# Two transformer stacks on one core: the RMS norms' sums of squares per token, in a 128x4 corner

## The reference

```python
def rmsnorm(x, g):
    xf = x.astype(jnp.float32)
    y = xf * lax.rsqrt(jnp.mean(xf * xf, axis=-1, keepdims=True) + EPS)
    return (y * g.astype(jnp.float32)).astype(x.dtype)
```

## Time and profile before

| | |
|---|---|
| median of 3 runs | 2605.52 us (2602.32 to 2605.62) |
| the profiled execution | 2600.53 us, of which the span from the first to the last instruction is 2598.8 us |
| PE busy | 2526.3 us (97%), 11928 matmul records |
| POOL busy | 1782.7 us (69%) |
| DVE busy | 1091.8 us (42%) |
| ACT busy | 578.7 us (22%) |

### The profile page before, as it was taken

One profiled execution on the slowest core, in us unless ns is written; L12 is line 12 of the kernel. 1 busy time (PEld: TensorE's weight loads), 2 busy tenths in 40 slices (PEclk: granted clock), 3 DMA queues, 4 the chain that ended last, 5 costly groups with the idle time before them and its releaser, 6 DMA issues.

```text
span 2598.8 us, 34640 instructions
## 1 busy us (share of the span) xinstructions
PE 2526.3 (97%) x11928; PEld 2032.1 (78%) x11928; DVE 1091.8 (42%) x1626; ACT 578.7 (22%) x992; POOL 1782.7 (69%) x816
## 2 busy tenths in 40 slices
PE   7999999999999899999999999989999999899999
PEld 5877778688888587777868888867888788688887
DVE  3565422544454366543254445456047732311100
ACT  2133222211100213331121111033224520211100
POOL 5766777588888376667758888825452467588887
PEclk9999999999999799999999999989999999999999
DMA  3222222222355122222223225511112122232233
GB/s 122 90 82 83 86 89 93 70 97 96 102 206 185 51 90 81 89 81 89 90 72 97 96 96 204 202 54 53 55 60 90 66 81 91 72 97 96 97 111 101
DMA packets 70213, 250.84 MB, mean 97 GB/s; under 512 B 8304, under 2 KB 8432, under 8 KB 70000
## 3 DMA queue, kind: packets, MB, share of 16 engines
q1 hardware_dynamic: 66816, 241.74, 28.1%
q10 hardware_dynamic: 3312, 7.95, 0.9%
HBM read 247.56 MB, written 2.10 MB: 96 GB/s over the span
## 4 chain that ended last, share of the span: by engine, by line
PE 64%; issue 13%; POOL 12%; DMA 9%; DVE 1%; SPq 0%; ACT 0%; POOLq 0%; DVEq 0%; ACTq 0%
PE bank L475 15%; PE bank L471 15%; PE bank L472 15%; DMA w_raw<-weights 9%; POOL w_lo L397 6%; POOL w_hi L394 5%; PE bank L425 3%; PE bank L426 3%; PE bank L427 3%; PE bank L699 1%; PE bank L1047 1%; PE bank L431 1%; PE bank L432 1%; PE bank L433 1%; PE bank L708 1%
## 5 line engine op out<-in xcount | busy, mean ns | idle before, releaser
L394 POOL TENSOR_TENSOR w_hi<-w_raw,one 128x1024 fp32r<-128x1024 f32 x405 | 778.0, 1921 | 775.2 <-PE bank L475 453.3
L397 POOL TENSOR_TENSOR w_lo<-w_raw,w_hi 128x1024 fp32r<-128x1024 f32 x405 | 1006.4, 2485 | 31.8
L471 PE MATMUL bank<-act_hi,w_hi 128*128 128x512 f32 x1840 | 726.5, 395 | 5.5 <-POOL w_hi L394 5.5
L472 PE MATMUL bank<-act_lo,w_hi 128*128 128x512 f32 x1840 | 717.6, 390 | 0.0
L475 PE MATMUL bank<-act_hi,w_lo 128*128 128x512 f32 x1904 | 472.3, 390 | 0.0
L475 PEld LDWEIGHTS bank<-act_hi,w_lo 128*128 128x128 f32 x1904 | 356.9, 188 | 74.8 <-issue 1.0
L471 PEld LDWEIGHTS bank<-act_hi,w_hi 128*128 128x128 f32 x1840 | 346.1, 188 | 85.6 <-issue 12.9
L472 PEld LDWEIGHTS bank<-act_lo,w_hi 128*128 128x128 f32 x1840 | 346.1, 188 | 75.1 <-issue 3.8
L471 PE MATMUL bank<-f_hi,w_hi 128*128 128x512 f32 x528 | 208.0, 394 | 0.0
L472 PE MATMUL bank<-f_lo,w_hi 128*128 128x512 f32 x528 | 208.0, 394 | 0.0
L475 PE MATMUL bank<-f_hi,w_lo 128*128 128x512 f32 x528 | 134.8, 394 | 0.0
(11 more groups left out here) (396 smaller groups left out, 3393.1 us busy)
## 6 DMA issues: line engine op xcount, KB each, us to landing
w_raw<-weights SPq DMA_DIRECT2D x405, 512.0 KB, 3.4
mod_raw<-mods SPq DMA_DIRECT2D x48, 512.0 KB, 4.3
bias<-bias ACTq DMA_DIRECT2D x8, 512.0 KB, 4.1
resid<-x SPq DMA_DIRECT2D x8, 256.0 KB, 5.2
out<-resid ACTq DMA_DIRECT2D x8, 256.0 KB, 4.2
params<-params ACTq DMA_DIRECT2D x2, 534.5 KB, 3.7
ctx_raw<-ctx SPq DMA_DIRECT2D x1, 1024.0 KB, 4.9
second<-second SPq DMA_DIRECT2D x1, 972.5 KB, 6.9
```

The source lines that it names most:

```text
L394: nc.gpsimd.tensor_tensor(w_hi[:, j, :], w_raw[:, j, :], one[:, 0:1].to_broadcast([P, 1024]), ALU.mult)\
L397: nc.gpsimd.tensor_tensor(w_lo[:, j, :], w_raw[:, j, :], w_hi[:, j, :].bitcast(F32), ALU.subtract).then_inc(blocks_split, 1)
L471: mm(out, w_hi[:, slot, tile * P:tile * P + P], rows_hi, start=start, stop=False)
L472: mm(out, w_hi[:, slot, tile * P:tile * P + P], rows_lo, start=False, stop=False)
```

## The change

The x norms get the y norms' form. `x_norm_sum` makes four fp32 matmuls of four columns in place of one of 512, with the squares as weights. Root and reciprocal are 128x4 (`root_x`, `rroot_x`). DVE builds the diagonals in `spread` and PE spreads them over the partitions with one more matmul (`x_norm_spread`). `apply` and `apply_mod` read the result from `bank[6]`; for the FFN's form ACT copies it to SBUF (`x_rstd_row`), where `ffn_scaled` waits for it. An identity is placed in `bank[7]` at each x norm. The context's sums move to `bank[4]`. In `add_rows` the next `scaled` is issued behind the addition and no longer ahead of it.

```diff
             def x_norm_sum(n, k):
 
+                if k == 0:
+                    nc.tensor.transpose(bank[7][:, P:2 * P], ident, ident).then_inc(x_ident, 1)
                 pe.wait_ge(x_sq, 8 * n + k + 1)
-                mm(bank[7][:, :], ones, squares[k % 2], start=(k == 0), stop=(k == KT - 1)).then_inc(x_summed, 1)
+                for tt in range(TT):
+                    last = mm(bank[7][:, 0:4], squares[k % 2][:, tt * P:tt * P + P], pick[:, 3 - tt:7 - tt],
+                              start=(k == 0 and tt == 0), stop=(k == KT - 1 and tt == TT - 1))
+                last.then_inc(x_summed, 1)
+
+            def x_norm_spread(n):
+
+                pe.wait_ge(x_spread, n + 1)
+                mm(bank[6][:, :], ones, squares[0], start=True, stop=True).then_inc(x_bc, 1)
...
                 first_two(b0, [bank[0][:, :], bank[1][:, :]], lo0, odd, norm=norm)
-                pairs(0, (2, 3))
+                pairs(0, (2,))
+                if norm is not None:
+                    x_norm_spread(norm)
+                pairs(0, (3,))
...
             x_norm_sums(0)
+            x_norm_spread(0)
...
                 mod_sums(28, 4).then_inc(mods_done, 1)
+                x_norm_spread(2 * l + 2)
...
             for k in range(KT):
-                last = mm(bank[6][:, 0:CTX], ones, ctx_sq[:, k, :], start=(k == 0), stop=(k == KT - 1))
+                last = mm(bank[4][:, 0:CTX], ones, ctx_sq[:, k, :], start=(k == 0), stop=(k == KT - 1))
...
             x_norm_sums(2 * DEPTH + 1)
+            x_norm_spread(2 * DEPTH + 1)
...
             def x_norm(n):
                 act.wait_ge(x_summed, 8 * n + 8 + 2)
-                run(root_row, bank[7][:, :], ACT.Sqrt, bias=eps, scale=1.0 / D).then_inc(x_root, 1)
+                run(root_x[:, 0:4], bank[7][:, 0:4], ACT.Sqrt, bias=eps, scale=1.0 / D).then_inc(x_root, 1)
+
+            def x_rstd_row(n):
+
+                act.wait_ge(x_bc, n + 1)
+                run(rstd_row, bank[6][:, :], ACT.Copy).then_inc(x_rstd, 1)
...
             def x_norm_later(n):
 
                 dve.wait_ge(x_root, n + 1)
-                step.inc(v.reciprocal(rstd_row, root_row))
-                return step.value()
+                did(v.reciprocal(rroot_x[:, 0:4], root_x[:, 0:4]))
+                dve.wait_ge(x_ident, n + 1)
+                v.tensor_tensor(x_diag, bank[7][:, P:2 * P].unsqueeze(1).to_broadcast([P, 4, P]),
+                                rroot_x[:, 0:4].unsqueeze(2).to_broadcast([P, 4, P]), ALU.mult).then_inc(x_spread, 1)
 
             def x_norm(n):
-                dve.wait_ge(step.sem, x_norm_later(n))
+                x_norm_later(n)
+                dve.wait_ge(x_bc, n + 1)
...
                 there = scaled(0)
                 for k in range(KT):
-                    following = scaled(k + 1) if k < KT - 1 else None
                     dve.wait_ge(step.sem, there)
                     v.tensor_tensor(resid[:, k, :], resid[:, k, :], tmp[:, k % 4, :], ALU.add).then_inc(x_ready, 1)
-                    there = following
-                    if then is not None and k >= 1:
-                        then(k - 1)
-                if then is not None:
-                    then(KT - 1)
+                    if k < KT - 1:
+                        there = scaled(k + 1)
+                    if then is not None:
+                        then(k)
```

More of the change, by code:

```diff
@@ L157, in build @@
         root_k, rroot_k = keep("root_k", [P, 48]), keep("rroot_k", [P, 48])
+        root_x, rroot_x = root_k[:, 0:4], rroot_k[:, 0:4]
         root_q, rroot_q, q_scale = keep("root_q", [P, 32]), keep("rroot_q", [P, 32]), keep("q_scale", [P, 8, TT])
@@ L215, in build @@
         sum_sq = tmp[:, 2, :]
-        rstd_row, root_row = squares
+        rstd_row = squares[0]
+        x_diag = spread[:, 0:4, :]
         KB = 1024
@@ L297, in build @@
         x_sq, x_summed, x_root = sem("x_sq"), sem("x_summed"), sem("x_root")
+        x_ident, x_spread, x_bc, x_rstd = (sem(n) for n in ("x_ident", "x_spread", "x_bc", "x_rstd"))
         t_ready, hi_ready, lo_ready = sem("t_ready"), sem("hi_ready"), sem("lo_ready")
@@ L1306, in _ @@
                 x_norm(2 * l + 1)
+                x_rstd_row(2 * l + 1)
                 ffn_scaled(BL * l + B_FFN, lambda b: use("ffn", b, 0, l), FT * l)
@@ L1320, in _ @@
             act.wait_ge(ctx_ss, 1)
-            run(root_row_c[:, :], bank[6][:, 0:CTX], ACT.Sqrt, bias=eps, scale=1.0 / D).then_inc(ctx_root, 1)
+            run(root_row_c[:, :], bank[4][:, 0:CTX], ACT.Sqrt, bias=eps, scale=1.0 / D).then_inc(ctx_root, 1)
             def apply_hi_mod(n, shift):
@@ L1562, in apply @@
                         dve.wait_ge(lo_ready, 8 * a + k - 3)
-                    v.scalar_tensor_tensor(tmp[:, k % 4, :], resid[:, k, :], g_pre[:, k:k + 1], rstd_row,
+                    v.scalar_tensor_tensor(tmp[:, k % 4, :], resid[:, k, :], g_pre[:, k:k + 1], bank[6][:, :],
                                            ALU.mult, ALU.mult).then_inc(t_ready, 1)
@@ L1594, in ffn_scaled @@
                         dve.wait_ge(f_lo_ready, f0 + 2 * i + j + 1)
-                        dve.wait_ge(step.sem, rstd_there)
+                        dve.wait_ge(x_rstd, rstd_there)
                         v.tensor_tensor(tmp[:, j, :], bank[2 * j][:, :], rstd_row, ALU.mult)\
@@ L1897, in _ @@
                 add_rows(G_POST_MIX, 16 * l + 8, rows_low)
-                rstd_there = x_norm_later(2 * l + 1)
-                ffn_scaled(rstd_there, BL * l + B_FFN, lambda b: use("ffn", b, 0, l), FT * l)
+                x_norm_later(2 * l + 1)
+                ffn_scaled(l + 1, BL * l + B_FFN, lambda b: use("ffn", b, 0, l), FT * l)
                 dve.wait_ge(f_lo_ready, FT * l + FT + 2)
@@ L1932, in apply_mod @@
                         dve.wait_ge(lo_ready, 8 * a + k - 3)
-                    v.scalar_tensor_tensor(tmp[:, k % 4, :], resid[:, k, :], gain[:, k:k + 1], rstd_row,
+                    v.scalar_tensor_tensor(tmp[:, k % 4, :], resid[:, k, :], gain[:, k:k + 1], bank[6][:, :],
                                            ALU.mult, ALU.mult).then_inc(t_ready, 1)
```

## The result

The changed kernel takes 2622.75 us (median of 4, 2620.34 to 2627.36) against 2603.92 us (median of 4, 2601.86 to 2605.62): a ratio of 1.0075, 95% interval 1.0056 to 1.0093, so it is slower by some 19 us. The prediction was 2625.6 us. The profiled execution took 2627.36 us with a span of 2625.6, 26.8 more than the span of before. It is the slowest of its four, and the profiled execution of before, at 2600.53 us, is faster than the four that its median is taken from, so the two traces lie further apart than the medians do.

The account below looks back on a forecast made before the run. The prediction took PE's stream, with POOL's splitting as partner, to bound the kernel. Terms 3.3 + 3.8 + 2.6 + 5.0 + 5.4 gave +20.1 us, 2625.6 us against the median; 8 in 10 between 2608 and 2642.

Parts of the forecast that it names:

- x norm 2: End of the first layer: sums stay at 1.2 GHz to the end, plus 3.5; chain minus 0.2; +3.3 us in all.
- x norm 0: Start: all eight sums at 1.2 GHz, plus 4.5; chain after them minus 0.7; +3.8 us in all.
- x norm 5: Second block's FFN: half the sums at 0.95, half at 1.71, plus 3.0; chain minus 0.4; +2.6 us in all.
- x norm 4: End of the second layer: slower sums plus 5.9, earlier addition minus 0.5, later context sums plus 1.1, clock minus 1.5; +5.0 us.
- x norms 1 and 3: First block's FFNs: earlier start -0.9, spreading +0.95, identity +0.15, weight loads +0.4, later clock rise +2.1; +2.7 us each.
- The cover that I named: In the first block's FFNs, blocks 2 and 3 cover the banks' later freeing; without it up to 4 us each.
- One sign of being wrong: The prediction is wrong if the FFNs' stretches at 0.50 last over 10 us.
- the second: Rival, same or faster, chance 0.14: PE's being busy is enough, clock goes its old way or better; 2602 or 2594 us.
- The third rival: Slower by far, chance 0.14: clock stays low until `first_two` is over in one or both FFNs; 2639 or 2652 us.
- the fourth: Rival, little slower, chance 0.08: sums at the start and second block's FFN stay at 2.4 GHz; about +10, 2615 us.

Follow-up runs that it names:

- e_ffn: The kernel before with the new form at the x norms in the two layers' FFNs alone, old order of `add_rows`; 2608.72 us, ratio 1.0016.
- e_wide32: As e_wide, but each piece of the x sums multiplies 32 columns of ones instead of 128, still into bank 4; 2617.28 us, ratio 1.0042.
- e_wide: The changed kernel with each piece of the x sums multiplying 128 columns of ones instead of 4 of `pick`, into bank 4; 2599.51 us, ratio 0.9973.
- e_wide_r: e_wide with squares and ones in float32r, 128 columns per piece; 2594.56 us, ratio 0.9951.
- e_onepass: The kernel before with the new order of `add_rows` and the squares and ones of the 512-column sums in float32r; 2584.94 us, ratio 0.9915.
- e_light1: The changed kernel with the squares and `pick` of the light x sums in float32r; 2591.59 us, ratio 0.9929.

## Why the prediction was right

It was right in sign and size, and in mechanism at the start, at the ends of the layers and at norm 5. In the FFNs I had taken one number for the clock's return, and the traces show a scatter. Against the sum of +20.1 us stand 18.8 by the medians, and 20.5 in the trace without the attention's stretch. That the two meet within half a us is partly luck: norm 3 came out 1.7 over its term, norm 5 0.3 over, and norms 0, 1 and 4 1.6 under theirs together.

- *x norm 2, +3.3*: +3.3. First sum to root 19.66 against the predicted 19.6, on 16.12. The chain gave back 0.36, predicted 0.2. Two things that the sum did not have cancel: the first sum starts 0.6 us earlier against the y norm than before (854.84 less 5.46 of lateness, for 849.99), because the clock had fallen later, and the return of the clock after the chain costs 0.8.
- *x norm 0, +3.8*: the sums 13.82 (predicted 13.7), the first `tmp` 3.8 after the root (predicted 3.96); it ends at +3.2, mainly because the clock is up earlier in the products behind it (3.4 us after the first one at 28.62, for 4.1 before). The reading of the clock set a load's duration, 0.34, against a spacing, 0.11; the loads of the same line at 2.4 GHz take 0.19, and the conclusion stands.
- *x norm 5, +2.6*: +2.9. The timeline of the changed kernel, for the earlier trace rows:

```profile
2237.71 11.24 PE L468 MATMUL bank<-pick,spread 128*128 128x4 f32 x64
...
2248.99 0.26 ACT L1184 ACTIVATE root_k<-bank,const 128x4 f32<-128x4 f32 x1 [1.42 <-PE bank L468]
...
2252.45 1.41 DVE L1959 SCALAR_TENSOR_TENSOR tmp<-resid,gain,bank 128x512 f32<-128x512 f32 x2 [2.17 <-PE bank L475]
```

The sums take 11.24 for the predicted 10.6; the clock fell at 2240.5, 2.8 us in. The chain takes 3.46 from root to `tmp` for the predicted 3.95. The two misses cancel.

- *x norm 4, +5.0*: +4.4. From the first sum to the root it is 20.02 us (1713.60 to 1733.62) for the predicted 19.6, and the sums start 1.2 us earlier, where I had taken 0.5. The context's sums start 3.4 us after the root, predicted 3.6 to 3.8, and take 4.46 for 5.38, since the clock rises within them, at 1738.7, behind the spreading. That the spreading brought it back is not shown:

```profile
1733.62 0.26 ACT L1184 ACTIVATE root_k<-bank,const 128x4 f32<-128x4 f32 x1 [4.49 <-PE bank L468]
...
1737.00 4.46 PE L812 MATMUL bank<-ctx_sq,const 128*128 128x256 f32 x16
```

- *x norms 1 and 3, +2.7 each*: +2.3 and +4.4. The parts are there in the timeline of the first (rows of PE, then of ACT and DVE):

```profile
471.25 0.79 PE L428 MATMUL bank<-act_hi,w_hi 128*128 128x512 f32 x1 [3.11 <-DVE act_lo L1920]
...
474.18 1.71 PE L468 MATMUL bank<-pick,spread 128*128 128x4 f32 x8
...
478.45 1.29 PE L468 MATMUL bank<-pick,spread 128*128 128x4 f32 x8
...
481.10 0.95 PE L468 MATMUL bank<-pick,spread 128*128 128x4 f32 x8
...
499.65 1.02 PE L475 MATMUL bank<-spread,const 128*128 128x512 f32 x2
500.11 0.79 PE L484 MATMUL bank<-act_hi,w_hi 128*128 128x512 f32 x1
```

```profile
500.71 0.60 ACT L1189 ACTIVATE spread<-bank 128x512 f32<-128x512 f32 x1 [6.96 <-PE bank L475]
```

```profile
501.40 0.69 DVE L1622 TENSOR_TENSOR tmp<-bank,spread 128x512 f32<-128x512 f32 x1 [6.72 <-ACT spread L1189]
```

PE's first product comes 0.9 us earlier after the y norm (471.25 less 3.2 of lateness, for 468.98), the spreading costs 0.9 between blocks 2 and 3, and the clock comes back 7.9 us after the first product for 3.8 before. That is the predicted 4 us, worth 2.1. At norm 3 it came back 12 us after the first product (1327.39 to 1339.3), and that is the term that I had too small: +4.4 for +2.7. How far light sums delay the return is not settled by this. At the six such visits to an FFN (changed kernel, e_ffn, e_wide32) it took 3.2 to 11.9 us from the first product, at the visits with the other forms 3.0 to 5.7. DVE's first read of bank 0 moved to 501.40 and not to 497, beyond the 501 at which I had PE ask for the bank; but PE is itself later, asks at 505.99, and finds it free: no step appears behind it in the comparison (from 510 to 830 us both run alike). The cover that I named held, with less to spare than I wrote.
- One sign of being wrong came true. I called the prediction wrong if the FFNs' stretches at 0.50 lasted over 10 us. They last 13.5 and 17. The sign was badly set, since the 10.1 of before already began ahead of `first_two`. But counted from PE's first product on it is 7.9 and 12, so at norm 3 it stands even then.

What I had only inferred, that the 512-column sums brought the clock back and the light ones don't, e_wide and e_wide32 show: same pieces, same bank, same price at one clock, 18 us apart by the columns alone. Columns alone are not enough, though: in float32r neither 128 nor 512 of them brought it back at the ends of the layers (e_wide_r, e_onepass). Of the rivals, the second describes e_wide and not the change. Its rule was that of the Trainium skill, page "TensorE: Matmul & The Clock Gate", Part 1. Taken by PE's busy time, that page doesn't fit these traces: in e_wide32 PE is busy 34.4 of 40.7 us and stays at 0.50, in e_wide it rises after 10.00 busy of 10.00, which would fit the page, and in the changed kernel 30.44 busy of 30.50 stay low, which does not. Its advice (section "Why this matters for your kernels") is to keep TensorE busy without gaps; here it was, and what it was busy with decided. The third rival (an FFN with 1.2 GHz until `first_two` is over, 13 us more than my sum) didn't happen; norm 3 exceeded its term by 1.7 of the 13. Nor did the fourth: the clock was at 0.50 through the sums of norm 0 and fell within those of norm 5.

The stretch in the attention was in no rival. The prediction was made from a profile without it, and it had to be told apart from the change before the profiled execution's 26.8 us could be read.

What stays open: why that stretch comes in some executions and in others of the same kernel not, and why the clock's return at one and the same place moves by several us from one kernel to the next (norm 3: +4.4 in the changed kernel, +1.3 in e_ffn, and the new order of `add_rows` should have made the changed kernel's the smaller).

## What to carry to other kernels

A matmul with few columns is not cheap on PE because it has little to do. Here four fp32 matmuls of four columns took about as long as one of 512 (0.95 and 1.02 us at 2.4 GHz), and after 2.8 us of them at norm 5 the rest ran at half the clock. Where a reduction over partitions must be made from small fp32 matmuls on PE's path, look up the granted clock beside them, count their records, and try wider columns at the same price; e_wide won 23 us over the changed kernel by 128 columns in place of 4. And before a profiled execution is compared stage by stage, check on a kernel that is unchanged there how much the stage moves by itself: here 6 us in one place and up to 1.2 in the others.

## What the runs showed of the hardware

- An fp32 piece (128x128 weights) is two records and costs nearly the same with 1, 4, 32 and 128 columns. A step of four such pieces and two `mod_sums` takes 2.56 us at 1.2 GHz with 4, with 32 (858.74 to 861.30) and with 128 columns. The row of the four pieces alone is 1.71 to 1.89 us long with 4 and 32 columns and 1.91 to 2.07 with 128, the end of the last one included; at 2.4 GHz it is 0.95 with 4 and 1.14 with 128.
- In float32r a piece is one record and costs 0.21 us at 1.2 GHz with four columns, half of the fp32 piece (e_light1). One 512-column sum in float32r takes 0.39 us at 2.4 GHz between products, in fp32 1.02.
- Float32 sums of 512 columns, or of pieces with 128, had the clock back at 2.4 GHz before they were over at 14 of 14 ends of layers, after 4 to 15 us of sums; float32 pieces of 4 or 32 columns and all float32r sums at none of 14.
- A stretch of 1.2 GHz appeared under matmuls that in other executions ran at 2.4 without a gap in PE's work, for 13.5 us, worth 6.2 us, in eight of the fourteen profiled executions (both kernels and twelve experiments, all with the same code there).
